# Selected-value pages gathered into a DRAM scratch during input panels 2 to 12, and loaded from there in eight blocks

## What is computed

```python
z = x @ lw['w_in']
u_conv, q_nsa, kv_nsa, g_nsa, qkv_moba, u_pool = jnp.split(z, IN_SPLITS, axis=-1)
y_conv, conv_new = conv_module(u_conv, conv_buf, ...)
o_cs = nsa_compressed_selected(qn, qpos, nsa_all, ...)
o_win = window_attend(qn, qpos, win_all[:, :, 0], win_all[:, :, 1], kpos)
o_moba = moba_attend(m[:, :, 0], qpos, moba_all[:, :, 0], moba_all[:, :, 1])
y_pool, pool_new = pool_mixer(u_pool, pool_buf, qpos, lw['pool_w'], lw['pool_scale'])
mix = jnp.concatenate([y_conv, o_nsa.reshape(b, t, -1), o_moba.reshape(b, t, -1), y_pool], axis=-1) @ lw['w_out']
```

```python
nsa_past = cache_nsa_kv[l, page_table].reshape(bs, past_len, 4, HEAD_DIM)
```

## Time and profile before

| | us |
|---|---|
| median of 3 runs | 768.87 |
| lowest, highest | 768.74, 770.88 |
| span of the profiled execution | 764.6 |
| busy in the span: TensorE | 736.4 (96%) |
| busy: DVE, ACT, POOL | 430.8, 285.5, 205.6 |
| input panels and what is among them | to 227 |
| stage behind the panels | 227 to 327 |
| output panels and feed-forward | from 327 |

### The profile page before, as it was taken

One profiled execution on the slowest core, in us unless ns is written; L12 is line 12 of the kernel. 1 busy time (PEld: TensorE's weight loads), 2 busy tenths in 40 slices (PEclk: granted clock), 3 DMA queues, 4 the chain that ended last, 5 costly groups with the idle time before them and its releaser, 6 DMA issues.

```text
span 764.6 us, 17340 instructions
## 1 busy us (share of the span) xinstructions
PE 736.4 (96%) x6904; PEld 658.4 (86%) x6904; DVE 430.8 (56%) x742; ACT 285.5 (37%) x561; POOL 205.6 (27%) x282
## 2 busy tenths in 40 slices
PE   8999999998988899999999999999999999999997
PEld 7999989875563455499999999999999999999996
DVE  4778994655644532558775556434553345536365
ACT  5222324455563222534425544212341234223125
POOL 0000527012326772005647712001110012100433
PEclk9999999999999899999999999999999999999999
DMA  9556773387699998132333323332333222325002
GB/s 333 180 158 181 214 201 104 122 287 297 235 314 328 265 272 268 65 99 68 117 137 98 90 83 111 111 89 79 91 104 101 93 83 84 111 83 165 2 15 100
DMA packets 63980, 113.49 MB, mean 148 GB/s; under 512 B 17017, under 2 KB 36218, under 8 KB 63226
## 3 DMA queue, kind: packets, MB, share of 16 engines
q1 hardware_dynamic: 57370, 95.58, 40.8%
q0 software_dynamic: 6528, 16.78, 6.6%
HBM read 107.90 MB, written 6.52 MB: 150 GB/s over the span
## 4 chain that ended last, share of the span: by engine, by line
PE 78%; DVE 9%; issue 4%; ACT 3%; DMA 3%; SPq 2%; POOL 0%; ACTq 0%; DVEq 0%
PE psum L790 55%; PE psum L809 4%; PE psum L817 3%; PE psum L896 2%; DMA moba_lo<-in_moba_pages 2%; PE psum L930 2%; PE psum L865 2%; PE psum L1083 2%; PE psum L1095 1%; DVE yc L1691 1%; DVE wL L1621 1%; SPq L629 1%; DMA wgate<-in_w_gate 1%; PE psum L1131 1%; DVE oxL L2045 1%
## 5 line engine op out<-in xcount | busy, mean ns | idle before, releaser
L1621 DVE TENSOR_TENSOR wL<-raw,wH 128x1024 fp32r<-128x1024 f32 (+1 forms) x87 | 109.5, 1259 | 88.4 <-ACT wH L1256 88.4
L1256 ACT ACTIVATE wH<-raw 128x1024 fp32r<-128x1024 f32 (+1 forms) x87 | 88.8, 1021 | 101.7 <-PE psum L790 100.5
L790 PE MATMUL psum<-oxH,wH 128*128 128x260 f32 (+1 forms) x512 | 105.0, 286 | 0.7 <-DVE oxL L2045 0.5
L790 PE MATMUL psum<-oxH,wL 128*128 128x260 f32 (+1 forms) x512 | 103.9, 284 | 0.0
L790 PE MATMUL psum<-oxL,wH 128*128 128x260 f32 (+1 forms) x512 | 103.4, 283 | 0.0
L1585 POOL TENSOR_TENSOR hsq<-relu 128x520 f32<-128x520 f32 x32 | 33.8, 1056 | 217.8 <-ACT relu L1435 217.8
L790 PE MATMUL psum<-opH,wH 128*128 128x260 f32 x400 | 85.2, 294 | 4.2 <-DVE wL L1621 1.4
L790 PEld LDWEIGHTS psum<-oxH,wH 128*128 128x128 f32 x512 | 79.5, 189 | 2.5 <-issue 1.7
L790 PE MATMUL psum<-opH,wL 128*128 128x260 f32 x400 | 80.5, 283 | 0.0
L790 PE MATMUL psum<-opL,wH 128*128 128x260 f32 x400 | 80.3, 282 | 0.0
L790 PEld LDWEIGHTS psum<-oxL,wH 128*128 128x128 f32 x512 | 79.9, 190 | 0.0
(11 more groups left out here) (394 smaller groups left out, 1306.5 us busy)
## 6 DMA issues: line engine op xcount, KB each, us to landing
raw<-in_panels SPq DMA_DIRECT2D x88, 512.0 KB, 3.6
nsa_ring<-in_nsa_pages SPq DMA_DIRECT2D x128, 96.0 KB, 2.2
moba_hi<-in_moba_pages SPq DMA_DIRECT2D x36, 256.0 KB, 5.6
moba_lo<-in_moba_pages SPq DMA_DIRECT2D x36, 256.0 KB, 6.1
moba_hi<-in_moba_pages POOLq DMA_DIRECT2D x28, 256.0 KB, 5.5
moba_lo<-in_moba_pages POOLq DMA_DIRECT2D x28, 256.0 KB, 6.0
xres<-in_xT SPq DMA_DIRECT2D x8, 260.0 KB, 5.5
xres<-in_xT SPq DMA_DIRECT2D x1, 2080.0 KB, 8.8
```

Source lines behind the costliest of these rows:

```text
L790: last = mm(out[:, hf, 0:cols], w, x[:, k, hf * HALF:hf * HALF + cols], start=(t == 0 and j == 0), stop=(t == KT - 1 and j == 2))
L1256: fn(wtiles(0, n).rearrange("p a b -> p (a b)")[:, cols], raw[:, n % NRAW, cols], ACT.Copy).then_inc(h_done, 1)
L1621: tt(wtiles(1, n).rearrange("p a b -> p (a b)")[:, cols], raw[:, n % NRAW, cols], wtiles(0, n).rearrange("p a b -> p (a b)")[:, cols].bitc ...
```

## The change

The 32 selected-value steps leave the stage behind the panels as page loads. In their place GpSimd issues 32 steps `gather`, two to four behind each of the panels 2 to 12, each when its panel's matmuls are done. A gather copies four pages into a scratch tensor in DRAM, in the layout that the product wants. Behind panel 16 SyncE loads one sample's 512 KB at a time from the scratch, the first after all gathers have landed, and the rest on due times of 1, 6, 11 and so on to 36 in the merged list. The product waits for one DMA instead of sixteen. In the list the gathers of a panel stand ahead of its taps, of `("pdiff", 0)` at panel 8 and of `("pdiff", 1)` at panel 10. Three pairs of semaphores are also merged into one each, with the waits raised from 1 to 2; no wait is added or dropped by that, and it isn't shown in full.

```diff
-MB1, PAIR_T, SELV_T = 9, 9.1, 6
-SELV_POOL = (1, 3, 5, 7)
-SELV_AT = [8 * (_m // 8) + (_m % 8) // 2 + 4 * (_m % 2) for _m in range(4 * B)]
+MB1, PAIR_T, SELV_T = 9, 9.1, 5
+GATHER0 = 2
+GATHERS = (2, 2, 2, 3, 3, 3, 3, 3, 3, 4, 4)
...
         if b == B - 1:
             tl.append(("load_post", 0))
+        if GATHER0 <= i < GATHER0 + len(GATHERS):
+            tl += [("gather", k, i) for k in range(sum(GATHERS[:i - GATHER0]), sum(GATHERS[:i - GATHER0 + 1]))]
         if i in (1, 6):
             tl.append(("glu", i // 6))
...
-        units += [(at_ + 4.6 * (m >= 4), ("selv", k)) for m, k in enumerate(SELV_AT[SELV_T * (g - MB1):SELV_T * (g - MB1 + 1)])]
     end = 1 + PAIR_T * (MB - MB1)
+    units += [(1 + SELV_T * b, ("selv", b)) for b in range(B)]
...
+        selv_rows = nc.dram_tensor("selv_rows", [B, P, PAGES, HD], F32, kind="Internal").ap()
...
-                elif kind == "selv" and n // 4 not in SELV_POOL:
+                elif kind == "selv":
                     if n == 0:
                         sp_.wait_ge(mm_done, N_IN_PANELS)
-                    for p, v in enumerate(pages(4 * n, 4), 4 * n):
-                        sp_.dma_start(selV[p // PAGES][:, p % PAGES, :],
-                                      a["selv_pages"][bass.ds(v, 1)].rearrange("a p n -> (a p) n")).then_inc(selv_in[p // PAGES], 16)
+                    if n == 0:
+                        sp_.wait_ge(selv_gathered, 16 * PAGES * B)
+                    sp_.dma_start(selV[n][:, :, :], selv_rows[n]).then_inc(selv_in[n], 16)
...
-                    pe.wait_ge(cact, 1)
+                    pe.wait_ge(cswish, 2)
...
-                    pe.wait_ge(selv_in[b], 16 * PAGES)
+                    pe.wait_ge(selv_in[b], 16)
...
-                if kind == "selv" and n // 4 in SELV_POOL:
-
-                    if n == 4:
-                        pool.wait_ge(mm_done, N_IN_PANELS)
-                    pool.wait_ge(mp_mm, MB1 + SELV_AT.index(n) // SELV_T - 1)
+                if kind == "gather":
+                    if n == 0:
+                        pool.wait_ge(ids_in, 16)
+                    pool.wait_ge(mm_done, part[0] + 1)
                     for p, v in enumerate(pool_pages(n * 4), n * 4):
-                        pool.dma_start(selV[p // PAGES][:, p % PAGES, :],
-                                       a["selv_pages"][bass.ds(v, 1)].rearrange("a p n -> (a p) n")).then_inc(selv_in[p // PAGES], 16)
+                        pool.dma_start(selv_rows[p // PAGES][:, p % PAGES, :],
+                                       a["selv_pages"][bass.ds(v, 1)].rearrange("a p n -> (a p) n")).then_inc(selv_gathered, 16)
```

More of the change, by code:

```diff
@@ L583, in build @@
             sem("shift_h"), sem("cq_done"), sem("cexp_done"), sem("pv_done"), sem("o_done"), sem("pick_done"))
+        selv_gathered = sem("selv_gathered")
         pool_d, pool_mm = sem("pool_d"), sem("pool_mm")
-        cm_mm, csq_done, cv_mm, cn_done, cth, cact, cpw_mm = (
-            sem("cm_mm"), sem("csq_done"), sem("cv_mm"), sem("cn_done"), sem("cth"), sem("cact"), sem("cpw_mm"))
+        cm_mm, csq_done, cv_mm, cn_done, cswish, cpw_mm = (
+            sem("cm_mm"), sem("csq_done"), sem("cv_mm"), sem("cn_done"), sem("conv_tanh_then_product"), sem("cpw_mm"))
         bfree = [sem(f"bank_free{k}") for k in range(4)]
-        csc_mm, csc_exp, csc_done, ctr_mm, ctr_done, cimp_mm = (
-            sem("csc_mm"), sem("csc_exp"), sem("csc_done"), sem("ctr_mm"), sem("ctr_done"), sem("cimp_mm"))
-        win_mm, win_exp, win_l = sem("win_mm"), sem("win_exp"), sem("win_l")
+        csc_mm, csc_probs, ctr_mm, ctr_done, cimp_mm = (
+            sem("csc_mm"), sem("csc_exp_then_scaled"), sem("ctr_mm"), sem("ctr_done"), sem("cimp_mm"))
+        win_mm, win_probs = sem("win_mm"), sem("win_exp_then_sums")
         ms_mm, mmax, mt_mm, mp_mm, om_done = (
@@ L1046, in _ @@
                     bank(1, step)
-                    pe.wait_ge(csc_done, 1)
+                    pe.wait_ge(csc_probs, 2)
                     for c in range(2):
@@ L1100, in _ @@
                     if n == 0:
-                        pe.wait_ge(win_l, 1)
+                        pe.wait_ge(win_probs, 2)
                     for s, src in enumerate(stats[n]):
@@ L1366, in _ @@
                     act.wait_ge(cn_done, 1)
-                    fn(zT[:, S_CG:S_CG + 2, :], yc[:, :, :], ACT.Tanh, scale=0.5).then_inc(cth, 1)
+                    fn(zT[:, S_CG:S_CG + 2, :], yc[:, :, :], ACT.Tanh, scale=0.5).then_inc(cswish, 1)
                 elif kind == "cpw":
@@ L1373, in _ @@
                     bank_read(act, 0, step)
-                    fn(Pc[:, :, 0:NCMP], Pc[:, :, 0:NCMP], ACT.Exp).then_inc(csc_exp, 1)
+                    fn(Pc[:, :, 0:NCMP], Pc[:, :, 0:NCMP], ACT.Exp).then_inc(csc_probs, 1)
                 elif kind == "cimp":
@@ L1380, in _ @@
                     bank_read(act, 1, step)
-                    fn(Pwin[:, :, :], Pwin[:, :, :], ACT.Exp).then_inc(win_exp, 1)
+                    fn(Pwin[:, :, :], Pwin[:, :, :], ACT.Exp).then_inc(win_probs, 1)
                 elif kind == "mu":
@@ L1532, in _ @@
                 if kind == "mp" and 2 * n + 5 < MU:
-                    if n == 0:
-                        pool.wait_ge(ids_in, 16)
                     q = 2 * n + 5
@@ L1748, in _ @@
                     last.then_inc(cn_done, 1)
-                    dve.wait_ge(cth, 1)
-                    stt(yc[:, :, :], zT[:, S_CG:S_CG + 2, :], 1.0, yc[:, :, :], ALU.add, ALU.mult).then_inc(cact, 1)
+                    dve.wait_ge(cswish, 1)
+                    stt(yc[:, :, :], zT[:, S_CG:S_CG + 2, :], 1.0, yc[:, :, :], ALU.add, ALU.mult).then_inc(cswish, 1)
                 elif kind == "csc":
@@ L1756, in _ @@
                     tt(Pc[:, :, 0:NCMP], s, spread(nmC, NCMP), ALU.add).then_inc(bfree[0], 1)
-                    dve.wait_ge(csc_exp, 1)
+                    dve.wait_ge(csc_probs, 1)
                     chain(red(lC, Pc[:, :, 0:NCMP], AX.X, ALU.add))
                     chain(nc.vector.reciprocal(lC, lC))
-                    tt(Pc[:, :, 0:NCMP], Pc[:, :, 0:NCMP], spread(lC, NCMP), ALU.mult).then_inc(csc_done, 1)
+                    tt(Pc[:, :, 0:NCMP], Pc[:, :, 0:NCMP], spread(lC, NCMP), ALU.mult).then_inc(csc_probs, 1)
                 elif kind == "ctr":
@@ L1792, in _ @@
                 elif kind == "winsum":
-                    dve.wait_ge(win_exp, 1)
-                    red(lW, Pwin[:, :, :], AX.X, ALU.add).then_inc(win_l, 1)
+                    dve.wait_ge(win_probs, 1)
+                    red(lW, Pwin[:, :, :], AX.X, ALU.add).then_inc(win_probs, 1)
                 elif kind == "mu":
```

## The result

| us | before | changed |
|---|---|---|
| median (22 runs each) | 767.01 | 770.56 |
| lowest | 762.54 | 766.94 |
| span of the profiled execution | 764.6 | 775.5 |
| its mean granted clock | 0.992 | 0.979 |

The ratio is 1.0053, with a 95% interval of 1.0033 to 1.0073: slower by 4.1 us (0.0053 x 767; the two medians alone differ by 3.6), where 9.7 were forecast. The direction was right and the range of 768.5 to 790 held the time, but the case's own range of 774 to 784 did not.

The account below looks back on a forecast made before the run. TensorE, busy 91.1 of 100 us behind the panels, was taken as the bound. Stall 7.4, contention 0.7, clock 2.5, ScalarE -0.7 and relieved queues -0.2 gave +9.7: 778.6 us, range 768.5 to 790, the case's own 774 to 784.

Parts of the forecast that it names:

- The cause: Panels 8 to 10: gathers ahead of GpSimd's second pooling pass make it end after TensorE reaches its product.
- Part 1: Behind the panels: 64 page issues each leave SyncE and GpSimd, 8 loads come; -0.2 us, bounds 0 and 5.3.
- part 2: Panels 8 to 12: gathers at 2.7 us each delay GpSimd's pooling passes; TensorE stalls 7.4 us at the second product.
- 0.7 for contention: Late second pooling pass beside four two-input DVE instructions: +0.7 us, between -1.2 and +2.8.
- The arrival of TensorE: TensorE comes to the second pooling product at 133.43 us, as in the kernel before.
- The clock, +2.5: Behind TensorE's stall the granted clock falls to its lower level: 2.5 us of work lost, between 1.7 and 3.4.
- ScalarE's wait at panel 13, -0.7: Start of panel 13: ScalarE and DVE catch up during the stall, so TensorE's 0.69 us wait goes: -0.7 us.
- The DMA engines, 0: In the panels: gathers take 2.4 to 3.6 us of all 16 engines a panel, but nobody waits: 0 us.
- Rival B: Panels 5 to 10: gathers fill the DMA engines and NSA pages come late; 788 us, chance 0.11.
- Rival A: Panels 8 to 10: GpSimd issues slower beside a busy DVE, 3.6 us a gather; 787 us, chance 0.10.
- Rival C: Second pooling product: gathers of 1.88 us or less cause no stall; 763.6 to 768.7 us, chance 0.13.
- The base: Whole kernel: median 768.87 us, 4.3 us above the profiled span of 764.6; the forecast adds its sum to 768.9.

Follow-up runs that it names:

- Blocks alone: Kernel before without its page loads: no gathers, SyncE loads eight 512 KB blocks from the weight panels' array; 766.59 against 766.46 us, ratio 0.9999.
- gathers alone: Kernel before, its 128 page loads behind the panels kept, with the changed kernel's gathers added at their places; 769.83 us, ratio 1.0055.
- e1_behind: Changed kernel with the gathers of panels 8 and 10 put behind the pooling passes in GpSimd's order; 769.63 us, ratio 1.0053.

## Why the prediction was right and wrong

- **The cause: right.** Nine gathers ahead of the second pass move it past TensorE's arrival. With four of them moved out of the chain the cost is gone; more of them cost much more; memsets in their place move the product as they do, though that kernel's time grew by more than its product moved.
- **Part 1, -0.2: right.** Blocks alone measured 0.9999. The wait of 0.21 us is gone.
- **The chain of part 2, the stall of 7.4 us with 0.7 for contention: the step that failed, by its size.** The path is the forecast one, but the term of 8.1 us measured 4.5 (product at 137.90 instead of 133.43). The second pass was to end at 141.5 with the contention and ended at 137.8. Four parts make the difference:
  - Nine gathers at 2.7 us are 24.3 us, and they took 7.4 + 14.7 = 22.1: -2.2. A full four cost 2.60 us and not 2.68, and the first eight DMAs behind the pass follow each other without the 0.40 us gap between groups (4.18 us).
  - The first of them starts at 83.44 and not at 82.8: +0.6. So the start of the first pass, 90.84 against 90.9, is right by luck, since a late start and cheaper gathers cancel.
  - The first pass takes 14.05 us instead of 15.3, beside other DVE work than before: -1.2.
  - The second takes 18.15 instead of 18.45 + 0.7: -1.0. The contention term was -0.3: the 504-wide addition took 1.25 us and no longer 2.27, and the last two instructions took 0.7 more together.

  Nine times an error of some 0.25 us is what a chain does to an estimate, and the two passes were priced with the neighbours that they had before.
- **The arrival of TensorE: not asked.** I took 133.43 for where TensorE stands as fixed. It comes at 135.42, because the first pass moved beside the convolution's taps, which lost 2.8 us. I costed the contention as time of the second pass alone and looked only at the four DVE instructions beside it. That loss isn't added to the stall but lies inside it: GpSimd decides when the product starts. It is why TensorE waits 2.5 us and not 4.5, and not why the forecast of the time was too large. Of the 4.9 us between the forecast wait and the measured one it is 2.0, and the shorter chain the rest.
  The rule of the Trainium skill (SBUF — State Buffer, Who interferes with whom) speaks of both engines, whoever comes first. The trace agrees with it on DVE's side as well: 1.78 us against 0.76 for the one instruction at 136.53. I had drawn only the half of it that concerned GpSimd.
- **The clock, +2.5: too large, and not a constant.** The profiled execution lost 1.7 us behind the stall; gathers alone, with the same stall of 2.5 us, lost nothing there. Over all executions it is about 1.5 us, an estimate: the 4.1 us less the 2.4 to 2.7 that remain at one clock. The two rows that I took it from were single executions too.
- **ScalarE's wait at panel 13, -0.7: right.** It is gone.
- **The DMA engines, 0: right, from a wrong price.** I had 38 to 58 us of one engine a panel for the gathers. The share in 61 to 72 us rose by 0.08, which is 0.08 x 11 x 16 = 14 us. Rival B had nothing to stand on. The Trainium skill's statement on transfers under 512 B (DMA: Bandwidth & Descriptors, Specifications), which a DMA engine reads, modifies and writes, speaks for a dearer write than I took from the loads into SBUF. No run shows a cost of it in the time.
- **Rival A: wrong way.** A page's DMA takes 528 ns of GpSimd on average, beside a busy DVE as in the stage of the earlier trace rows. Rival C's place was right, a margin that depends on the time of a gather, and its end of the range was nearer than mine.
- **The base.** I put 4.3 us around the span. In every run the time is about 1.7 us above its own span, so the profiled execution of before was one of 766.3 us, and the rest is the spread between executions. It didn't enter the difference. And the bounds that I named add up to 775.9 to 781.6 us; the own range of 774 to 784 was drawn wider than they are.

Summed again with what was measured: 4.5 for the product, up to 1.7 for the clock, -0.7 for ScalarE: 3.8 to 5.5, where the forecast had 9.7. The chain is 3.6 of the difference, the clock 0.8 and more. Panel 13 is 4.9 us late, the MoBA product at 229.12 is 4.3, the runs say 4.1.

No version tried beats the kernel before. The best has five gathers in the chain and none ahead of the first pass (0.9995), and gives nothing for the work that it takes from the stage behind the panels, since no wait there hangs on it.

## What to carry to other kernels

Work moved to an "idle" engine is put into that engine's order: compute the end of each result that stands behind it against the moment when its reader comes, and count the moved units there, since an error in one is multiplied by their number. Then move the reader too: ask which instructions of the neighbouring engine the shifted work now runs beside, and what these hold up. And where the stage that is relieved has no wait on what is taken away, the best outcome of the change is no change.

## What the hardware showed that was not expected

- **The spread between executions goes with the mean clock.** The executions of the changed kernel reach from 766.94 us at a clock of 0.993 to 777.41 at 0.981. The same stall was followed by a clock of 0.50 to 0.88 in one profile and of 1.00 in another. An effect of 4 us can't be read from two single profiles whose spans differ by 10.9.
- **A gap at one place of GpSimd's DMAs.** In all eight kernels with gathers the 114th of their 128 DMAs comes late: here by 3.11 us, in six others by 2.96 to 3.39, in run e1_behind by 6.84, though it lies at different moments (139.7 to 157.6 us). Behind the first gather no other waits more than 0.8 us for "issue". The cause wasn't looked for.

```profile
151.28 0.53 POOL L1548 DMA_DIRECT2D selv_rows<-in_selv_pages  x1 [3.11 <-issue]
```

- **Gathers into DRAM in runs of 256 bytes were cheap.** 128 page DMAs cost GpSimd 67.4 us in all and no measurable time of the kernel where they stood out of the chain.
